# Modulation pieces laid as 2 column halves by 64 row blocks, a group summed by 8 tiles and a half-picking matrix

## The reference, cut to what matters

```python
# first block, twice (DEPTH = 2)
mod = c_act @ ada_w[l] + ada_b[l]          # c_act: 2048, ada_w[l]: 2048 x 6144
shift, scale, gate = split(mod, 3)         # three groups of 2048
h = rms_norm(x, norm_g[l]) * (1.0 + scale) + shift
...                                        # latent attention, convolution
x = x + gate * y
# second block, once
mod = silu(c_2) @ w_ada_2 + b_ada_2        # 2048 x 12288: six groups of 2048
sh1, sc1, ga1, sh2, sc2, ga2 = split(mod, 6)
```

## Time and profile before

| | |
|---|---|
| median of the 3 runs | 2408.45 us |
| span of the profiled execution | 2405.4 us |
| TensorE busy | 2242.7 us (93%) |
| VectorE busy | 1791.1 us (74%) |
| ScalarE busy | 924.6 us (38%) |
| mean granted TensorE clock | 0.966 |
| moved by the DMA engines | 557.39 MB, mean 232 GB/s |
| the SyncE queue, q1 | 550.70 MB, 69.3% of 16 engines |
| pieces of the modulation | 384 x 512 KB = 201 MB, VectorE 484.9 us |
| sums over the partitions (L1493, L1507) | 56.9 us of TensorE |

### The profile page before, as it was taken

The page is one execution under the profiler, slowest core; times in us unless marked ns, Lnnn a source line. Parts: engine busy times, 40 slices in busy tenths (PEclk is TensorE's granted clock), DMA queues, the critical chain, the costliest instruction groups (busy, mean ns, idle before and its releaser), DMA issues.

```text
span 2405.4 us, 41562 instructions
## 1 busy us (share of the span) xinstructions
PE 2242.7 (93%) x16273; PEld 2137.8 (89%) x16273; DVE 1791.1 (74%) x2404; ACT 924.6 (38%) x1355; POOL 52.6 (2%) x63
## 2 busy tenths in 40 slices
PE   3299999998989998999999999899999999999998
PEld 2298997788989977899999997689999999999998
DVE  6897998797979987978867867768885656644444
ACT  2154404224634042354443432255543444434343
POOL 0000000000000000023000000000000000000000
PEclk7599999999999999999999999899999999999998
DMA  9988955696988466959948984257875555555553
GB/s 336 361 277 284 304 150 201 226 326 199 309 282 283 137 232 216 333 156 273 370 145 300 360 299 151 95 168 251 275 257 166 183 183 183 183 158 182 180 185 108
DMA packets 413233, 557.39 MB, mean 232 GB/s; under 512 B 25139, under 2 KB 362103, under 8 KB 412868
## 3 DMA queue, kind: packets, MB, share of 16 engines
q1 hardware_dynamic: 409536, 550.70, 69.3%
q0 software_dynamic: 1120, 2.18, 0.5%
q10 hardware_dynamic: 2468, 3.07, 0.4%
HBM read 553.72 MB, written 2.17 MB: 231 GB/s over the span
## 4 chain that ended last, share of the span: by engine, by line
PE 77%; DVE 10%; DMA 7%; issue 4%; ACT 2%; SPq 0%; DVEq 0%; ACTq 0%
PE gemm L1473 70%; DMA w_raw<-in_w_in 4%; DVE ada_acc L994 2%; DMA ada_first<-in_ada_w 2%; PE stat L1493 2%; DVE w_lo L1026 1%; ACT w_hi L708 1%; PE bankO L1544 1%; DVE ss L1221 1%; DMA ada_raw<-in_w_ada 1%; DVE ada_acc L1013 0%; PE bankS L1647 0%; PE bankS L1646 0%; DVE q_tok L1228 0%; DVE k_tok L1228 0%
## 5 line engine op out<-in xcount | busy, mean ns | idle before, releaser
L1026 DVE TENSOR_TENSOR w_lo<-w_raw,w_hi 128x1024 fp32r<-128x1024 f32 (+1 forms) x564 | 675.6, 1210 | 391.2 <-ACT w_hi L708 388.1
L1473 PE MATMUL gemm<-h_hi,w_hi 128*128 128x256 f32 (+2 forms) x3056 | 871.3, 285 | 19.2 <-DVE h_lo L1071 13.9
L1473 PE MATMUL gemm<-h_hi,w_lo 128*128 128x256 f32 (+2 forms) x3056 | 868.5, 284 | 0.0
L1473 PE MATMUL gemm<-h_lo,w_hi 128*128 128x256 f32 (+2 forms) x3056 | 868.4, 284 | 0.0
L708 ACT ACTIVATE w_hi<-w_raw 128x1024 fp32r<-128x1024 f32 (+1 forms) x564 | 571.8, 1028 | 650.1 <-PE gemm L1473 540.1
L1473 PEld LDWEIGHTS gemm<-h_hi,w_hi 128*128 128x128 f32 (+2 forms) x3056 | 587.4, 192 | 21.0 <-issue 16.5
L1473 PEld LDWEIGHTS gemm<-h_lo,w_hi 128*128 128x128 f32 (+2 forms) x3056 | 587.5, 192 | 0.5
L1473 PEld LDWEIGHTS gemm<-h_hi,w_lo 128*128 128x128 f32 (+2 forms) x3056 | 587.2, 192 | 0.3
L994 DVE SCALAR_TENSOR_TENSOR ada_acc<-ada_raw,c_act,ada_acc 128x1024 f32<-128x1024 f32 x288 | 364.2, 1278 | 5.6 <-DMA ada_raw<-in_w_ada 3.0
L1473 PE MATMUL gemm<-G_hi,w_hi 128*128 128x256 f32 x704 | 200.7, 285 | 3.1 <-DVE w_lo L1026 3.1
L1473 PE MATMUL gemm<-G_hi,w_lo 128*128 128x256 f32 x704 | 200.4, 285 | 0.0
(11 more groups left out here) (294 smaller groups left out, 2703.8 us busy)
## 6 DMA issues: line engine op xcount, KB each, us to landing
w_raw<-in_w_in SPq DMA_DIRECT2D x264, 512.0 KB, 5.7
w_raw<-in_w_up SPq DMA_DIRECT2D x176, 512.0 KB, 3.6
ada_raw<-in_ada_w SPq DMA_DIRECT2D x160, 512.0 KB, 6.9
ada_raw<-in_w_ada SPq DMA_DIRECT2D x160, 512.0 KB, 5.1
w_raw<-in_w_out SPq DMA_DIRECT2D x96, 512.0 KB, 6.3
w_raw<-in_w_down SPq DMA_DIRECT2D x64, 512.0 KB, 3.7
ada_first<-in_ada_w SPq DMA_DIRECT2D x32, 512.0 KB, 8.8
ada_late<-in_w_ada SPq DMA_DIRECT2D x32, 512.0 KB, 4.3
```

The lines of the kernel that those rows point to most:

```text
L1026: dve.tensor_tensor(w_lo[:, fixed % PARTS, 0:sz], w_raw[:, fixed % RAW, 0:sz], w_hi[:, fixed % PARTS, 0:sz].bitcast(F32), ALU.subtract).th ...
L1473: last = pe.matmul(half(g, k, q), left, right, start=(kt == 0 and j == 0), stop=(u == len(g.units) - 1 and t == nk - 1 and j == len(parts) ...
```

## The change

A piece now holds 1024 columns of both halves at once: the 128 partitions are 2 halves of the columns (c) by 64 blocks of rows (k), `"(k j) (c n) -> c k j n"` with j = 32. Partition 64c + k holds, in piece j, the columns of half c of row 32k + j. There are still 32 pieces of 512 KB in a group, and a group's sum is 128 x 1024. The sum over the partitions takes 8 tiles against halves_of, a 128 x 128 matrix whose columns 0 and 1 pick the partitions 0 to 63 and 64 to 127; two columns of `stat` remain of each tile, and mod is read from them in a permuted order. The groups 0 and 1 keep two sums of 1024 columns each (pieces j even and odd) and are summed by 16 matmuls as before, two to a tile.

In the program the source pattern of a load changes from 128 rows (step 98304 elements, that is 16 rows) of 1024 elements to 2 (step 1024) by 64 (step 196608, that is 32 rows) of 1024 elements; the outermost count is 2 instead of 128. On the side of the on-chip memory it is 128 partitions by 1024 before and after. c_raw is loaded by four loads of 64 x 32 instead of two of 128 x 16.

```diff
-AU = KT * GROUP // AC
+CB2 = GROUP // AC
+AU = DM * CB2 // P
+AC_T = AC // P
...
-GAP_FIRST = 6
+GAP_FIRST = 3
...
-        ada_acc = at("ada_acc", W0 + 16, [P, GROUP])
-        ada_acc1 = at("ada_acc1", 80, [P, GROUP])
+        ada_acc = at("ada_acc", W0 + 16, [P, AC])
+        c_raw = at("c_raw", W0 + 20, [P, 2, AU])
+        c_act = at("c_act", W0 + 20.25, [P, 2, AU])
+        halves_of = at("halves_of", W0 + 20.5, [P, P])
+        ada_acc1 = at("ada_acc1", 80, [P, 2 * AC])
+        ada_acc0 = at("ada_acc0", 88, [P, 2 * AC])
...
+        def rows_of(n):
+
+            w, grp, _ = groups[n]
+            return w[:, grp * GROUP:(grp + 1) * GROUP].rearrange("(k j) (c n) -> c k j n", j=AU, c=CB2)
...
-                w, grp, _ = groups[n]
-                slot, c0 = (AU * n + j) % FSLOTS, grp * GROUP + j % 2 * AC
-                src = w.rearrange("(p m) n -> p m n", m=KT)[:, j // 2:j // 2 + 1, c0:c0 + AC]
-                sp.dma_start(first_slot(slot), src).then_inc(ada_loaded[slot], 16)
+                slot = (AU * n + j) % FSLOTS
+                sp.dma_start(first_slot(slot), rows_of(n)[:, :, j:j + 1, :]).then_inc(ada_loaded[slot], 16)
...
-                w, grp, _ = groups[n]
-                slot, c0 = fixed % ASLOTS, grp * GROUP + fixed % 2 * AC
-                src = w.rearrange("(p m) n -> p m n", m=KT)[:, bass.ds(m, 1), c0:c0 + AC]
+                slot = fixed % ASLOTS
+                src = rows_of(n)[:, :, bass.ds(m, 1), :]
                 sp.dma_start((ada_late if n == 11 else ada_raw)[:, slot:slot + 1, :], src).then_inc(ada_loaded[slot], 16)
...
-                slot, acc = fixed % ASLOTS, acc_of(n)[:, fixed % 2 * AC:(fixed % 2 + 1) * AC]
+                slot, acc = fixed % ASLOTS, acc_of(n)[:]
                 dve.wait_ge(ada_loaded[slot], rounds * 16)
-                if n or j >= 2:
-                    dve.wait_ge(ada_used, j + (AU * n - 1))
+                dve.wait_ge(ada_used, j + AU * n)
...
-                for t in range(KT):
-                    last = pe.matmul(stat[:, t:t + P], acc[:, t * P:(t + 1) * P], ones[:], start=True, stop=True)
+                n_acc = acc.shape[1] // AC
+                for t in range(AC_T):
+                    for j in range(n_acc):
+                        last = pe.matmul(stat[:, CB2 * t:CB2 * t + P], acc[:, j * AC + t * P:j * AC + (t + 1) * P],
+                                         halves_of[:], start=(j == 0), stop=(j == n_acc - 1))
```

More of the change, by code:

```diff
@@ L128, in program @@
         eps_t = at("eps_t", 118 + 64 / 1024, [P, 1])
-        c_raw = at("c_raw", 118 + 96 / 1024, [P, 2, KT])
-        c_act = at("c_act", 118 + 224 / 1024, [P, 2, KT])
         negmax = at("negmax", 118 + 352 / 1024, [P, HEADS_AHEAD, TT])
@@ L193, in program @@
         va_tok = at("va_tok", B1 + 32, [P, TT, DC])
-        ada_acc9 = at("ada_acc9", B1 + 48, [P, GROUP])
+        ada_acc9 = at("ada_acc9", B1 + 48, [P, AC])
         oaT = at("oaT", B1 + 40, [P, CT, T])
@@ L418, in acc_of, with by_half, summed_halves @@
         def acc_of(n):
-            return {1: ada_acc1, 9: ada_acc9}.get(n, ada_acc)
+            return {0: ada_acc0, 1: ada_acc1, 9: ada_acc9}.get(n, ada_acc)
+        def by_half(x):
+            return x.rearrange("p (c j) -> p c j", c=CB2)
+        def summed_halves(x):
+            return x[:, 0:KT].rearrange("p (j c) -> p c j", c=CB2)
+        def rows_of(n):
+            w, grp, _ = groups[n]
+            return w[:, grp * GROUP:(grp + 1) * GROUP].rearrange("(k j) (c n) -> c k j n", j=AU, c=CB2)
         def none(i, k):
@@ L516, in ada_pieces @@
             fixed = [j0 + f for v in units_beside(before, u, units) for f in range(math.ceil(v * each), math.ceil((v + 1) * each))]
-            return [(n, i * per + f, i * (per // 2) + f // 2, f, i * (per // ASLOTS) + ((AU * (n - 2) + f) // ASLOTS + 2 * AU // FSLOTS + 1))
+            return [(n, i * per + f, i * per + f, f, i * (per // ASLOTS) + ((AU * (n - 2) + f) // ASLOTS + 2 * AU // FSLOTS + 1))
                     for f in fixed]
@@ L587, in _ @@
             pool.memset(eps_t[:], EPS)
+            link(pool.memset(halves_of[:], 0.0))
+            for c in range(CB2):
+                link(pool.memset(halves_of[c * DM // AU:(c + 1) * DM // AU, c:c + 1], 1.0))
             pool.memset(ones[:], 1.0).then_inc(ones_done, 1)
@@ L664, in link @@
                 act.wait_ge(act_step, steps[0])
-            act.dma_start(c_raw[:, 0, :], a["c"][0].rearrange("(p m) -> p m", m=KT)).then_inc(c_loaded, 16)
-            act.dma_start(c_raw[:, 1, :], a["c_2"][0].rearrange("(p m) -> p m", m=KT)).then_inc(c_loaded, 16)
+            for n, v in enumerate((a["c"], a["c_2"])):
+                for c in range(CB2):
+                    act.dma_start(c_raw[c * DM // AU:(c + 1) * DM // AU, n, :],
+                                  v[0].rearrange("(k j) -> k j", j=AU)).then_inc(c_loaded, 16)
             act.dma_start(x_tok[:], a["x"][0].rearrange("(t p) n -> p t n", p=P)).then_inc(x_loaded, 16)
-            act.wait_ge(c_loaded, 32)
+            act.wait_ge(c_loaded, 16 * 2 * CB2)
             act.activation(c_act[:], c_raw[:], ACT.Silu).then_inc(silu_done, 1)
@@ L1001, in mod_out @@
                 b = groups[n][2]
-                ins = dve.tensor_tensor(mod[:, n, :], stat[:, 0:KT], par[:, b:b + KT], ALU.add)
+                ins = dve.tensor_tensor(by_half(mod[:, n, :]), summed_halves(stat), by_half(par[:, b:b + KT]), ALU.add)
                 ins.then_inc(stat_read, 1)
@@ L1012, in ada_start @@
                         dve.wait_ge(ada_used, j + (AU * n - 1))
-                    dve.scalar_tensor_tensor(out=acc, in0=first_slot(slot)[:, 0, :], scalar=c_act[:, 0, j // 2:j // 2 + 1],
+                    dve.scalar_tensor_tensor(out=acc, in0=first_slot(slot)[:, 0, :], scalar=c_act[:, 0, j:j + 1],
                                              in1=acc, op0=ALU.mult, op1=ALU.add).then_inc(ada_used, 1)
@@ L1056, in norm @@
                     b = groups[GAP_MOD[r]][2]
-                    link(dve.tensor_tensor(mod[:, GAP_MOD[r], :], bankO[:, 0:KT], par[:, b:b + KT], ALU.add))
+                    link(dve.tensor_tensor(by_half(mod[:, GAP_MOD[r], :]), summed_halves(bankO), by_half(par[:, b:b + KT]), ALU.add))
                 if scale is not None:
@@ L1506, in mod_tiles @@
                     for t in ts:
-                        last = pe.matmul(bankO[:, t:t + P], ada_acc[:, t * P:(t + 1) * P], ones[:], start=True, stop=True)
+                        last = pe.matmul(bankO[:, CB2 * t:CB2 * t + P], ada_acc[:, t * P:(t + 1) * P], halves_of[:],
+                                         start=True, stop=True)
                     return last
@@ L1521, in norm @@
                 if r in GAP_MOD:
-                    mod_tiles(range(GAP_FIRST, KT)).then_inc(gap_summed, 1)
+                    mod_tiles(range(GAP_FIRST, AC_T)).then_inc(gap_summed, 1)
             def tr_bank(n):
```

## The result

The changed kernel takes 5513.54 us, the median of 4 runs (5512.78 to 5517.16), against 2409.67 us for the kernel before beside it. The ratio is 2.2881, with a 95% interval of 2.2848 to 2.2913. It is slower by 3104 us; 5520 were forecast.

A forecast was written before the change was run, and what follows sets the result against it. TensorE was taken to bound most of the span, with loads close behind in stages with pieces. 656 + 3824 + 1140 - 84 = 5536 us, less 16 for the sums, gave 5520 us; range 5050 to 6000.

The forecast's parts named there:

- a piece on two fixed engines: Loads of pieces: each runs on the same two engines, 10.25 us a piece instead of 1.28; chance 0.84.
- a unit of weights, beside it: Weight loads in stages with pieces: a unit's 32 KB on each slow engine takes 1.70 us of its time.
- first stage, to the last addition: Groups 0 and 1 at the start: 64 pieces at 10.25 us, 656 us instead of 110.
- the other 320 pieces: Later stages with pieces: 320 pieces with as many units, 10.25 + 1.70 us each, 3824 us.
- all else, sums included: Stages without pieces stay bound by TensorE, 1140 us, less 16 us for the sums over the partitions.
- the overlap at the crossings: Loads gain while TensorE still works on a stage without pieces: some 12 us at 7 crossings, -84 us.
- The sums: Sums over the partitions: seven groups go from 16 tiles to 8, -16 us; norms 2 us at most.
- The wait of an addition: VectorE additions standing together: 0.11 us a pair, at most 56 pairs, 6 us uncovered; nothing in the sum.
- waking up: TensorE after each slow stage: waking at the lower clock might add 50 us; allowed for in the range.
- Sixteen engines: Rival on the loads of pieces: all 16 engines still serve a piece, 2395 us, faster; chance 0.10.
- One engine: Rival on the loads of pieces: one engine for a piece, as for dw_rows, 9460 us; chance 0.02.
- Changing pairs: Rival on the loads of pieces: two engines, but others for each load, 2433 us; chance 0.04.

The follow-up runs named there:

- outer2: Kernel before with only its pieces' and c's row blocks reordered, so the source has 2 outermost; sums and waits unchanged: 5520.07 us, ratio 2.293.
- outer4: Kernel before with only its pieces' and c's row blocks reordered, so the source has 4 outermost: 3757.79 us, ratio 1.561.
- outer8: Kernel before with only its pieces' and c's row blocks reordered, so the source has 8 outermost: 3008.77 us, ratio 1.250.
- interleaved version: Changed kernel with partitions numbered 2k + c instead of 64c + k, so the source has 64 outermost: 2402.25 us, ratio 0.9967 against the kernel before.
- pair_wait: Kernel before with each of the 320 later additions also waiting for the addition right before it: 2413.53 us, ratio 1.0014.

## Why the prediction was right
The mechanism was the one forecast, and the time lies 6 us off. Both are not equally well earned. The sum had three errors of up to 110 us, of which two cancelled; that only 6 us are left is luck. What is earned is the number of engines and the price of a piece, within 3%. By its steps:

| step | forecast us | measured us |
|---|---|---|
| a piece on two fixed engines | 10.25 | 9.98 |
| a unit of weights, beside it | 1.70 | 1.46 |
| first stage, to the last addition | 656 | 665 |
| the other 320 pieces | 3824 - 84 = 3740 | 3630 |
| all else, sums included | 1140 - 16 = 1124 | 1221 |
| total | 5520 | 5515 |

The fourth row is the time from first to last addition of the seven stretches: 535 + 524 + 526 + 526 for 48 pieces each, 363 for 32, 739 for 64 and 417 for 32. The fifth is what is left of the span.

*Two fixed engines.* Right; outer2, outer4 and outer8 show the count alone at work. That the 31 rows of dw_rows gave one engine was the best row for it; that 2 rows give two engines was read into it and is now measured. A piece did cost less than 10.25 us, but not because 14 engines idle: with 2, 4 and 8 engines each moves the same 26.2 GB/s, and a packet of 4 KB lasts 159 ns (median) in 84 to 104 us of the kernel before as well as of the changed one. The forecast's 0.164 us came from counting the whole share to the large packets, with 250 small ones among 2249; here 4 of 262 are small.

*The pieces, 110 us too dear.* The two durations are 320 x (0.27 + 0.24) = 163 us too long. The pace of units, 19.3 GB/s, came from a busy share that counts the whole queue; 32 KB in 1.46 us are 22 GB/s. Against that stands the overlap at the crossings: -84 us were forecast, and 320 x 11.44 - 3630 = 31 us is all that can be seen of it. The measured prices give five of the seven stretches back within 8 us: 48 pieces with 32 units are 479 + 47 = 526 us (524 and 526 measured), 32 with 32 units 366 (363), 64 with 64 units 732 (739), 32 with 64 units 319 + 93 = 413 (417). For lat to ub, 48 pieces with 48 units, they give 549 us, and 535 and 526 were measured.

*All else, 97 us too cheap.* The same cut through the kernel before gives 1223 us: its first stage ends at 109.8 us, and its seven stretches of additions take 1072.2 us. So this part did not move, as forecast but for the 16 us of the sums. But the windows of the earlier trace rows count as stages with pieces what lies between two groups of pieces there: the norms, the sums, and the units ahead of the first piece. With the boundaries set at the first and last addition instead of at stages, the sum would have been 656 + 3824 + 1223 - 84 - 16 = 5603 us, 90 too many. A window should be cut at the instructions whose pace it prices.

*First stage, 9 us too short.* By the measured price the 64 pieces are 639 us, and the stage ends at 665: 26 us are missing, and the price of 10.25 hid 17 of them. They lie at the start, where the fourth addition begins at 63.0 us and from there on one every 9.98 us. The prediction had guessed 10 us for x_tok and the constants on the two engines and left them out. All of their 3.09 MB move in these first 60 us; which of them holds the pieces up was not taken apart.

*The sums.* Forecast -16 us for seven groups, 2 in the norms. In the changed kernel this can't be seen behind 3000 us; in the interleaved version it is -13.4. *The wait of an addition:* at nothing there, behind the loads; 3.4 us in pair_wait, of 6 at most.

*TensorE.* Its busy time grew by 502 us at the lower clock, and the total doesn't show it: in the chain TensorE keeps 0.20 x 5515 = 1103 us, less than the 1221 us that are not loads of pieces. The 50 us kept for waking up were not needed: the last stage, 4911 to 5515 us, lasts 604 us against 603.

*The signs.* The additions wait for the loads, the first stage is long and the last stage keeps its length, as forecast. One sign was put wrongly: a DMA share near 0.12 in the stages with pieces. It is 12.9% only where pieces move alone; from lat to ub it is 0.28 and from q to outcb 0.23, since the units there are still spread over all 16 engines.

*The rivals.* Sixteen engines: excluded by 12.9% and 53 GB/s; its time, 2395 us, is nearly what the interleaved version reaches (2402), where the layout does get all engines. One engine: it would have been half the GB/s. Changing pairs: the first stage would have ended near 110 us, and it ended at 665.

## What to carry to other kernels
Look at the outermost count of a load's source before its bytes (the destination kept its 128 here): 2, 4 and 8 gave as many of the 16 engines, and an exchange of two dimensions of the layout (64 outermost instead of 2) turned +3104 us into -8. Spread each load over all the partitions and keep the outermost count at 32 or more, where the full pace was measured: full engines at 238 GB/s are as real a loss as idle ones, and only the GB/s beside the share show it, in more than one window. In a sum by stages, take the price of a step from the distance between two of its instructions, and cut the stages at these instructions; otherwise errors of a hundred microseconds can hide each other.

## What the runs showed of the hardware that was not expected
- 16 outermost rows over 128 partitions keep 16 engines 97% busy at 250 GB/s; 32 give 413 GB/s, 64 give 408.
- 8 outermost rows gave 210 GB/s in group 0 and 134 in group 1 (outer8), at the same share of 51.2%.
- Pieces in two loads to 64 neighbouring partitions each run at 58% of the pace (238 against 408 GB/s), though each load has 64 rows outermost.
- The issue of a load on SyncE took 4.5 to 6.6 us (695 to 718 us) instead of 0.34 with two engines behind.
- Fewer columns in the short sums made them no faster (1.84 against 1.95 us) while the kernel was 12 us slower, at a mean granted clock of 0.959 instead of 0.969.
